# One block per expert with loads issued ahead of the routing, and routing steps of both token halves alternated

## The reference, cut to what matters

```
# _hier_moe: t = 256 tokens, 8 groups of 8 experts, 2 experts a token
g_p, g_idx = top_k(softmax(xt @ w_grp + b_grp), 1)
el_sel = (xt @ w_er + b_er) of the group g_idx            # 8 logits
e_p, e_loc = top_k(softmax(el_sel), 2);  e_p /= sum(e_p)
e_glob = g_idx * 8 + e_loc;  weights = g_p * e_p
# for each token and each of its experts e:
out += weight * (silu(x @ w1[e]) * (x @ w3[e])) @ w2[e]   # 1024 -> 512 -> 1024
```

## Time and profile before

| | us |
|---|---|
| median of 3 runs | 2967.42 (2966.04 to 2968.5) |
| the profiled execution's own time | 2967.49 |
| its span, first to last instruction | 2965.7 |
| PE busy | 2269.8 (77%) |
| DVE busy | 1128.3 (38%) |
| ACT busy | 716.7 (24%) |
| POOL busy | 34.4 (1%) |

### The profile page before, as it was taken

One profiled execution on the slowest core, in us unless ns is written; L12 is line 12 of the kernel. 1 busy time (PEld: TensorE's weight loads), 2 busy tenths in 40 slices (PEclk: granted clock), 3 DMA queues, 4 the chain that ended last, 5 costly groups with the idle time before them and its releaser, 6 DMA issues.

```text
span 2965.7 us, 32146 instructions
## 1 busy us (share of the span) xinstructions
PE 2269.8 (77%) x12773; PEld 1618.0 (55%) x12773; DVE 1128.3 (38%) x2026; ACT 716.7 (24%) x1040; POOL 34.4 (1%) x56
## 2 busy tenths in 40 slices
PE   7998879855766666566664877879899877788899
PEld 5875558722322232222321644568899644567899
DVE  1678846421000010000101366643563356633653
ACT  2134435300000000000000234431452224421552
POOL 0000000000000000000000100000000100000000
PEclk8998989967778888777776887889899987889999
DMA  8433424189999999999997131123443431123352
GB/s 313 144 117 139 147 80 158 46 332 421 422 422 421 422 422 422 422 422 422 422 422 287 29 122 43 42 96 112 149 160 125 135 111 43 57 86 128 133 193 101
DMA packets 177968, 644.14 MB, mean 217 GB/s; under 512 B 11201, under 2 KB 29153, under 8 KB 128657
## 3 DMA queue, kind: packets, MB, share of 16 engines
q1 hardware_dynamic: 173008, 628.07, 54.1%
q10 hardware_dynamic: 2304, 8.39, 0.7%
q0 software_dynamic: 2496, 5.48, 0.6%
HBM read 630.37 MB, written 11.53 MB: 216 GB/s over the span
## 4 chain that ended last, share of the span: by engine, by line
PE 49%; DMA 28%; DVE 15%; ACT 5%; issue 3%; SPq 2%; DVEq 0%; POOL 0%; ACTq 0%; POOLq 0%
DMA ring<-in_w 25%; PE pb L171 22%; PE pb L970 3%; PE pb L987 3%; PE pb L1686 3%; PE pb L1687 3%; PE pb L1688 3%; DVE ar L2099 3%; DVE parts L1766 2%; DVE ar L686 2%; PE pb L1629 2%; PE pb L1652 2%; SPq L905 1%; PE pb L196 1%; PE pb L482 1%
## 5 line engine op out<-in xcount | busy, mean ns | idle before, releaser
L171 PE MATMUL pb<-ar,ring 128*128 128x256 f32 (+1 forms) x2960 | 714.7, 404 | 31.3 <-DVE ar L1946 13.2
L171 PEld LDWEIGHTS pb<-ar,ring 128*128 128x128 f32 (+1 forms) x2960 | 590.5, 202 | 156.2 <-issue 43.4
L970 PE MATMUL pb<-ring,ar 128*32 128x512 f32 x2048 | 307.8, 758 | 186.3 <-DMA ring<-in_w 174.5
L1686 PE MATMUL pb<-act,parts 128*128 128x256 f32 x1152 | 333.9, 290 | 22.6 <-DVE act L2099 15.5
L1687 PE MATMUL pb<-act,parts 128*128 128x256 f32 x1152 | 328.9, 286 | 0.0
L1688 PE MATMUL pb<-act,parts 128*128 128x256 f32 x1152 | 328.8, 285 | 0.0
L970 PEld LDWEIGHTS pb<-ring,ar 128*32 128x32 f32 x2048 | 81.7, 134 | 399.9 <-issue 383.5
L987 PE MATMUL pb<-ring,ar 128*32 128x512 f32 x1024 | 177.2, 855 | 118.0 <-DMA ring<-in_w 118.0
L1686 PEld LDWEIGHTS pb<-act,parts 128*128 128x128 f32 x1152 | 224.4, 195 | 25.9 <-issue 18.7
L1687 PEld LDWEIGHTS pb<-act,parts 128*128 128x128 f32 x1152 | 224.3, 195 | 0.6
L1688 PEld LDWEIGHTS pb<-act,parts 128*128 128x128 f32 x1152 | 224.1, 195 | 0.0
(11 more groups left out here) (298 smaller groups left out, 2316.6 us busy)
## 6 DMA issues: line engine op xcount, KB each, us to landing
ring<-in_w SPq DMA_DIRECT2D x384, 1024.0 KB, 19.8
ring<-in_w_in SPq DMA_DIRECT2D x36, 2048.0 KB, 8.1
ring<-in_w_ff SPq DMA_DIRECT2D x32, 2048.0 KB, 8.0
ring<-in_w_ada SPq DMA_DIRECT2D x12, 2048.0 KB, 11.9
ring<-in_w_ssm_out SPq DMA_DIRECT2D x4, 2048.0 KB, 8.6
yd<-ar ACTq DMA_DIRECT2D x16, 512.0 KB, 8.0
ring<-in_w_out SPq DMA_DIRECT2D x4, 2048.0 KB, 8.1
ring<-in_w_cv_out SPq DMA_DIRECT2D x2, 2048.0 KB, 7.9
```

The source lines that it names most:

```text
L171: ins = e.matmul(out, l, r, start=(i == 0), stop=(i == len(pairs) - 1))
L970: ins = e.matmul(k.pb[b][32 * j:32 * j + 32, :], v.xg[i][:, kt, 32 * j:32 * j + 32], w[j][:, m, :], start=(kt == 0), stop=(kt == 7))
L1686: e.matmul(k.pb[b][:, 0:T], wh[:, kt, c0:c0 + 128], xh, start=(first and kt == 0), stop=False)
```

## The change

`ve`, `pe`, `sp` stand for the streams of the functions `moe_ve`, `moe_pe` and `moe_sp`.

1. Block e belongs to expert e for e = 0 to 63. Its loads have a fixed address, and no table is read for them. Tokens of an expert past its 32nd go to further blocks from 64 on (`NMORE` = 16), which the sections handle. The section of quad q runs if the number of further blocks is above 4(q - 16).
2. SP no longer waits for the table. Loads 0 to 3 follow the router's weights without a wait, loads 4 to 7 wait for `mm_tail` 20, and 8 to 11 for `mm_tail` 24. `HOMES` reorders the slots so that the memory which comes free first is used first.
3. PE forms the logits first, two products as each of the 8 parts of `n2` comes, and transposes after that.
4. DVE's routing steps alternate between the token halves; each waits only for the step that it reads. The weights (L1113 to L1115) move behind quad 0.
5. A row number within the first 64 blocks is 32e plus the token's position in its expert. The block counts, for the further blocks alone, move into quads 0, 1 and 2, between `sel` and the copies of `xg`.

```diff
 def moe_sp(k, e):
     def quad(q):
-        xs = [e.value_load(k.tab[0:1, 4 * q + j:4 * q + j + 1], ...) for j in range(4)]
+        if q >= QUADS:
+            xs = [e.value_load(k.tab[0:1, 4 * (q - QUADS) + j:...], ...) for j in range(4)]
...
                     if n >= HALVES:
                         e.wait_ge(*used(n - HALVES))
+                    elif n >= 4 and n % 4 == 0:
+                        e.wait_ge(*k.at("mm_tail", 20 if n == 4 else 24))
+                    w = a[name][4 * q + j:4 * q + j + 1] if q < QUADS else a[name][bass.ds(xs[j], 1)]
...
-    e.wait_ge(*k.at("mm_tail", 24))
-    e.wait_ge(*k.at("table", 2))
     for q in range(QUADS):
         quad(q)
+    e.wait_ge(*k.at("table", 2))
     in_sections(k, e, quad)
 
 def in_sections(k, e, quad):
     for q in range(QUADS, NBLK // 4):
-        count = e.value_load(k.tab[0:1, NBLK:NBLK + 1], min_val=0, max_val=NBLK)
-        with e.If(count > 4 * q):
+        count = e.value_load(k.tab[0:1, NMORE:NMORE + 1], min_val=0, max_val=NMORE)
+        with e.If(count > 4 * (q - QUADS)):
             quad(q)
             e.wait_ge(*k.at(f"y_stored{q % 2}", 16 * (q // 2 + 1)))
 
 def moe_pe(k, e, emptied):
+    e.wait_ge(*k.at("w_rt", 16))
+    lg = [ring.take(("lg", tt)) for tt in range(2)]
+    for i in range(8):
+        e.wait_ge(*k.at("n2", i + 1))
+        for tt in range(2):
+            ins = e.matmul(k.pb[lg[tt]][:, 0:72], v.n2[:, i, ...], v.wr[:, i, :], start=(i == 0), stop=(i == 7))
+    ins.then_inc(k.s("mm_rt"), 1)
...
     for tt in range(2):
         b = ring.take(("place", tt))
-        pairs = [(k.con("before"), v.asg[:, tt, :]), (ones[0:64, :], v.dg)] + [(ones, v.asg[:, 0, :])] * tt
+        e.wait_ge(*k.at("asg", tt + 1))
+        pairs = [(k.con("before"), v.asg[:, tt, :])] + [(ones, v.asg[:, 0, :])] * tt
...
     def quad(q):
+        if q == 0:
+            e.wait_ge(*k.at("nt", 4))
...                                                   # xg of both halves
+        if q in (1, 2):
+            count_more(q)
 
 def moe_ve(k, e, o):
+    t = [o.done(o.after(t[tt]).max(v.gm[:, tt, :], lg[:, tt, 0:8])) for tt in both]
+    t = [o.done(o.after(t[tt]).max_index(v.gi[:, tt, :]..., v.gm[:, tt, :], lg[:, tt, 0:8])) for tt in both]
...                                                   # the same steps as before, in pairs
+    t = [o.done(e.tensor_scalar(v.base[:, tt, :], v.ef[:, tt, :], float(BLKROWS), None, ALU.mult)) for tt in both]
+    for tt in both:
+        e.wait_ge(*k.at("place", tt + 1))
+        p = k.pb[k.bank["place", tt]][:, 0:64].unsqueeze(1).to_broadcast([128, 2, 64])
+        u.append(o.done(e.tensor_tensor(v.ppr[:, tt, :, :], v.oh[:, tt, :, :], p, ALU.mult), k.s("pos")))
+    u = [... tensor_reduce(v.pos[:, tt, :], v.ppr[:, tt, :, :], AX.X, ALU.add) ...]
+    u = [... tensor_scalar(v.far[:, tt, :], v.pos[:, tt, :], float(BLKROWS), None, ALU.is_ge) ...]
+    t = [... tensor_tensor(v.first[:, tt, :], v.pos[:, tt, :], v.base[:, tt, :], ALU.add) ...]
+    for tt in both: ... scalar_tensor_tensor(v.first, v.far, 65536.0, v.first, ALU.mult, ALU.add)
+    def count_more(step):
+        e.wait_ge(*k.at("counted", step + 1))
+        # step 0: 3 operations, over = (32 * [1..7] < count), blocks past the first
+        # step 1: 4 operations; step 2: 2 for the table, 12 for dst, 1 for its index
     def quad(q):
+                place = (v.first if q < QUADS else v.dst)[:, tt, j:j + 1]
...                                                   # sel
+        if q in (0, 1, 2):
+            count_more(q)
```

More of the change, by code:

```diff
@@ L69, in __init__, with after @@
         self.e, self.sem, self.count, self.last = e, sem, {}, None
-    def after(self):
-        if self.last is not None:
+    def after(self, *results):
+        for r in results:
+            self.e.wait_ge(*r)
+        if not results and self.last is not None:
             self.e.wait_ge(*self.last)
@@ L81, in done @@
         self.last = (sem, n)
+        return self.last
 class Ring:
@@ L932, in moe_pe @@
[L932 to L940, removed]
@@ new lines, in moe_pe @@
+    k.group(e, k.pb[more][0:64, 0:1], [(v.asg[:, i, :], ones[:, 0:1]) for i in range(2)]).then_inc(k.s("counted"), 1)
+    def count_more(step):
+        p = k.pb[more]
+        e.wait_ge(*k.at("blocks", step))
+        if step == 1:
+            k.group(e, p[0:64, 2:3], [(k.con("upto")[0:64, :], v.nb)]).then_inc(k.s("counted"), 1)
+        else:
+            e.matmul(p[0:1, 4:4 + NMORE], ones[0:64, 0:1], v.cmp, start=True, stop=True)
+            e.matmul(p[0:1, 4 + NMORE:5 + NMORE], v.nb, ones[0:64, 0:1], start=True, stop=True)
+            e.matmul(p[:, 64:128], ones[0:64, :], v.dg, start=True, stop=True).then_inc(k.s("counted"), 1)
+            ring.until(more, *k.at("dst_index", 1))
@@ L1082, in moe_ve @@
     inv = inverse(k, o, ROOT["h"])
+    o.after()
     for i in range(8):
[L1084 to L1115, removed]
@@ L1135, in moe_ve @@
-    o.done(o.after().tensor_copy(v.idx.bitcast(U32), v.dst), k.s("dst_index"))
+        o.done(e.scalar_tensor_tensor(v.n2[:, i, :], k.h[:, i, :], g2[:, i:i + 1], inv, ALU.mult, ALU.mult), k.s("n2_scaled"))
+    both = range(2)
+    one = [slice(tt, tt + 1) for tt in both]
+    e.wait_ge(*k.at("mm_rt", 1))
+    o.after()
+    t = [o.done(e.tensor_tensor(lg[:, tt, :], k.pb[k.bank["lg", tt]][:, 0:72], k.row("brt"), ALU.add), k.s("lg")) for tt in both]
+    t = [o.done(o.after(t[tt]).max(v.gm[:, tt, :], lg[:, tt, 0:8])) for tt in both]
@@ new lines, in moe_ve @@
+    u = [o.done(o.after(u[tt]).tensor_reduce(v.pos[:, tt, :], v.ppr[:, tt, :, :], AX.X, ALU.add)) for tt in both]
+    u = [o.done(o.after(u[tt]).tensor_scalar(v.far[:, tt, :], v.pos[:, tt, :], float(BLKROWS), None, ALU.is_ge)) for tt in both]
+    t = [o.done(o.after(t[tt], u[tt]).tensor_tensor(v.first[:, tt, :], v.pos[:, tt, :], v.base[:, tt, :], ALU.add)) for tt in both]
+    for tt in both:
+        o.done(o.after(t[tt]).scalar_tensor_tensor(v.first[:, tt, :], v.far[:, tt, :], 65536.0, v.first[:, tt, :], ALU.mult, ALU.add))
```

112 lines of the change are left out of this document (76 added, 36 removed).

## The result

The changed kernel takes 2993.47 us (median of four runs, 2992.45 to 2996.87) against 2967.96 before (2966.04 to 2969.2). The ratio is 1.0089, 95% interval 1.0071 to 1.0106: 25 us slower. The forecast was 3005 with a range of 2995 to 3019. The sign and its cause were right; the time lies 1.5 us under the range.

A forecast was written before the change was run, and what follows sets the result against it. The weights' DMA stream was taken to bound the quads, a third of the time. Sum: 2967.5 - 26.4 (earlier stream) + 61.2 (section) + 0.5 (entering) + 2 (behind it) = 3004.8, forecast 3005, range 2995 to 3019.

The forecast's parts named there:

- The sign and its cause: Whole kernel: slower (0.88), since one further block makes section 16 run a whole quad of 24 loads.
- The count: Router on its own inputs: expert 59 has 33 tokens, so one further block, section 16 runs, 408 loads.
- Part 1, the logits: PE's router products as `n2` arrives: 0.27 us each, two left after the last `n2`, done at 584.5 us.
- Part 1, the chain: DVE's routing up to the last `asg`: 10.44 us becomes 9.4; alternating saves 1.3 up to `sel`, bounds 0 and 3.
- Part 1, the sum: Earlier weight stream, at group 3: gain 26.4 us, 29.8 from the prefetch less 3.4 from a later restart; bounds 24 to 31.
- Part 2: Block counts moved into quads 0 to 2, ahead of the `xg` copies: cost 0; 5 us once if not hidden.
- The cover: At a quad's start DMA still has queued work: some 7 us free to hide the counts' 5 us in quad 2.
- Part 3, the section: Section 16 after the last quad: 24 loads and one store cost 61.2 us, entering 0.5, at most 8.
- Part 3, behind it: From the section's store to gather and next layer's loads: costs 2 us, bounds -4 and +6.
- POOL's checks: Three more section checks in front of POOL's gather: 2.4 us in the path.
- PE's dear skips: PE's checks of skipped sections after the store: 6.8 us each, three just in time for the next layer.
- rival (c): Routing and gather: alternation brings all a removed wait can, 2 us, and the gather runs free, 6: 2997; 10 in 100.

## Why the sign was right, and where the sizes failed

**The count.** 33 tokens for expert 59, one further block, 408 loads: as worked out from the router. (One reading in the prediction is slightly off: the 9s of the DMA row run from slice 10 to slice 21, and slice 9 is an 8. Nothing hangs on it.)

**Part 1, the logits.** Forecast 584.5, in the change's execution 586.7. Measured 588.68, 2.0 late. I took 0.27 us a product from products behind the transposes; at half the clock they took 0.42, more than the 0.59 us between arrivals allows for a pair.

**Part 1, the chain.** This was mis-sized. Alternating was priced at 1.3 us with a bound of 3. It was worth about 4.6: of an estimated 9.4 us to `asg`, 4.8 were left. I argued that an operation's time is its own, since hardly 0.03 us lie between end and start. That is no evidence: every one of those operations had waited for the one before, so their rows could not show how early one may start. The one pair without a wait pointed the right way. The two misses cancel in part: `sel` came 2.0 us earlier than forecast, and so did PE's start (607.40 against 609.4).

**Part 1, the sum.** Forecast 26.4. Taking off the 2.2, group 3 came 27.1 us earlier, and the last group of quad 15 29.1. The 2.0 of PE's start are in both. Against them, SP's reissue (611.10) gave data only 14.0 us later, where I had carried 12.8 over from the stream's first start, and this was made up again further on. From the reissue to the last group of quad 15 it is 951.8 us; before, from the first issue and less three groups, 952.6. So the pace of the stream gave 0.8 and not the 2 that a count from group 3 suggests.

**Part 2.** The cover held. DVE's copies of `xg` in quad 2 come late, PE starts that quad at 727.52, and the DMA share from 680 to 740 stays at 1.01 with 418 GB/s.

**Part 3, the section.** Forecast 61.2 + 0.5, measured 60.65, its edges hidden.

**Part 3, behind it: the term that failed.** I gave +2 with a bound of -4, and from the end of the last product to DVE's weighing it was -3.5 (21.35 against 24.86). I saw that the next layer's loads would start later and looked at the gather only, which hardly changed (10.80 us, before 11.07). The transfer that gained was the store: 8.28 us beside the loads, 2.60 without. POOL's checks cost what was forecast, but behind a store that took 5.7 us less. PE's dear skips stayed out of the way: the last ended at 1651.2, and PE was wanted at 1654.6. Holding the loads in the kernel before gave 3.3 us and a store 3.45 us shorter, so the loads are shown to cost that much; the section's store gained 2.2 more, and why is open.

Added up from the profiled executions: 2967.5 + 2.2 - 29.1 + 60.65 - 3.5 = 2997.7, measured 2996.87. Against the forecast that is 5.5 us in the term behind the section, 2.7 in the stream's start and pace, and 1 in the section. The 2 us that remain of the 11 between forecast and median are of the size of the scatter, and no trace of a median execution tells more. All lower bounds together had given 2994 and the range was set to begin at 2995; the median lies under both. It lies nearest to rival (c), 2997, which gave alternation all that a wait can bring and let the gather run free. Of that the first half came true and more; the second came from the store and not from the gather.

## What to carry to other kernels

A fixed assignment buys a prefetch but makes the worst bin decide: count what the data fill each bin with before pricing the schedule, for here one row of 512 cost as much as 24 MiB of weights. Fix only as many blocks as are needed to cover the time until the table is known, and pack the rest. Before a stream of loads is started beside a small transfer that everyone waits for, look when its first byte is needed.

## What the runs showed of the hardware that was not expected

- Two small DVE operations with no wait between them overlap: two maxima in 0.28 us against 0.17 for one and 0.20 to 0.21 from start to start with a wait; a chain of the same steps took 4.8 us alternated and 11.5 with every step waiting.
- A store of 512 KB landed 8.28 us after issue beside 7 MB of loads issued by another engine 0.8 us before it (8.05 and 8.61 in two more kernels). Without loads beside it, it took 3.6 to 5.0 in the four runs whose kernels hold them and 2.6 in the six that run a section.
- After 4.1 us of pause PE's granted clock fell to its lower level within the first us of the next products. In the change, whose products ran without a gap for 10 us and then with pauses of 1.7 and 2.9, it stayed there for 20 us. In the kernel before and with PE's old order it fell in the same way and was back at 1.00 some 7 us later. With the pause filled it stayed at the full level through the same products.
- The 16 logit products took 6.7 us at the lower level and 4.78 at the full one. The `xg` products took 7.88 and 7.67: a clock that is given back is not always time that is given back.
- An If that skips its section costs PE 3.8 to 7.6 us in the branch itself in the kernel before and 3.5 to 6.8 in the change, and the other engines under 0.1. PE's branch into the section took 0.09. The branch instructions of the changed kernel (least, median, most ns):

```profile
L890 POOLq COMPARE_BRANCH  x5: 38/45/50, 723.6 to 1634.5; - x5
L890 PEldq COMPARE_BRANCH  x5: 86/3475/6790, 1565.4 to 1644.4; - x5
```
